# GpSimd takes two products of VectorE in a hybrid decoder layer: the delta rule's gate and the rotation's sin

## The chip, the cores and the metric

One core of one Trainium2 chip runs the whole program. The metric is the device time of one execution in microseconds. Single numbers below come from one profiled execution, whose own time stands beside its span.

## The reference, cut to what matters

Two decoder layers run over 576 token columns: 512 of a prompt and 64 of eight sampled sequences. Each layer projects the normed input and feeds three token mixers: a gated linear recurrence (RG-LRU), sparse attention (NSA) and a gated delta rule. The change touches the output of the delta rule and the rotation of q and k of the attention.

```python
q = rope(rmsnorm(nsa_q...), pos) * HD ** -0.5        # 8 heads of 64
k = rope(rmsnorm(kv[:, :, 0::2], k_norm), pos)       # 3 branches, 2 heads of 64
# rope on the first 16 of each head's 64:
concat([x1 * c - x2 * s, x2 * c + x1 * s, rest])
...
o_dn = rmsnorm(o_dn, dn_o_norm)
out_dn = (o_dn * silu(dn_z)) @ w_dn_out
```

## The kernel before, in words

Columns of features lie on the 128 partitions and the 576 tokens along the free dimension, all in float32. Five engines run their own instruction lists and meet through semaphores.

TensorE carries one long list of dense units (`UNITS`, 288 token columns of one product each). Their order is fixed, and `fill(n, end)` strews n matmuls of it between the small matmuls of the mixers; each unit writes one of two PSUM banks in turn, so a unit can start only when the one two before it has been evicted. Weights are multiplied in a seven-product scheme (`PRODUCTS = "1627543"`): VectorE forms sums of weight quarters in SBUF (`weight_sums`, three instructions, after product 5; `weight_sum`, one instruction, after product 6), and both inputs of these lie in SBUF. VectorE evicts most units in `take_to(end)`, which handles all units up to `end`; `take_before(name, count)` evicts up to what TensorE had been given when it reached that step. Both are in order: what stands behind an instruction on VectorE waits for it.

Between the delta rule and attention each layer goes through this stretch:

- `times_roots` (L1984) multiplies the norms in, out of PSUM, for o (the delta rule's output, `dc[:, 0:4]`), then k (`qk7[:, 4:7]`), then q (`qk7[:, 0:4]`), each in two halves of 288 tokens. `bm_ok` counts them: 6 when o is done, 8 when k is, 10 when q is. TensorE's broadcasts for the next norm wait for them.
- GpSimd (L829 to L834) waits for `bm_ok` 8 and 10 and issues four DMAs each, which write the rows of k and q with the two rotation halves swapped into `rs7`. They count `nk_sw` and `nq_sw`.
- VectorE, after `bm_ok` 10, multiplies `zs[:, 8:12]` (the SiLU gate) with `dc[:, 0:4]`, 2304 elements per partition (`dn_ok`). Then for k (1728 elements) and q (2304): the swapped rows times sin, the rows times cos, and their sum (`qk_ok` 1 and 2), with evictions in between.
- TensorE waits for `bm_ok` 10, then for 16 matmuls of dense work later for `qk_ok` 1, and transposes k and v in five tiles with dense work in between (L864). ScalarE copies them out of PSUM to `ktok` (L1714), from where GpSimd writes them to DRAM (L840 to L848).
- SyncE loads the cached keys of the first samples after `dn_ok` and `qk_ok` 2 (L659).

The helpers that most instructions go through have lines of their own in the trace: `mul` is L1799, `add` L1802, `sub` L1805, matmuls of the dense list L935, transposes L864, norm broadcasts L981. `arena`, `zs`, `ring`, `ws`, `sg` and `con` are in SBUF, `PS` is PSUM; `dc`, `qk7`, `rs7` and the tables of sin and cos are parts of `arena`.

Of the kernel before, what the change touches and what calls it, by code (L numbers as in the profile page):

```python
# [16 lines left out]
ALU = mybir.AluOpType  # L17
# [278 lines left out]
NORMS = {"dn": (0, 4), "dn_k": (1, 4), "o": (2, 4), "k": (3, 3), "q": (4, 4)}  # L296


def chained(eng, done):
# [12 lines left out]
CON_IN = 16 * 3  # L312
# [7 lines left out]
qb_ok ck_in wk_in cv_in s_pl s_pe s_kt s_ke s_t s_ed s_ea s_sg s_sc s_pv s_cm s_ce  # L320
s_cn s_im s_wc s_m s_mw s_wm s_sm s_p s_pw s_tr s_tb s_ta s_mix s_or s_ot s_z dh_t
conv_ok silu_ok dc_ok sp_abs sp_exp gb_ok bm_ok s0_in p_z p_y p_g p_e p_x p_s p_d p_k p_b i_w
# [5 lines left out]
    par_in=192, lrow_in=48, par_t=1, ssq_ok=1, x_ps=1, rt_ok=5, rr_ok=5, xn_ok=5, x_t=9, sq_ok=19, ms_ok=5, rstd_ok=5,  # L328
    h_ok=9, lam_ok=1, lh_t=1, u_ok=4, lgp=8, lg=8, at_ok=1, lt_ok=1, lq_ok=1, lru_ok=1, lc_ok=1, lc_in=1, lo_t=2,
    lo_ok=3, gt_t=1, gt_ok=2, gs_ok=2, bc_ok=10, nk_sw=64, nq_sw=64, qk_ok=2, kt_t=5, kt_e=5, vc_mm=1, c_ok=1, c_s=4,  # L330
    c_m=4, c_e=4, c_t=4, c_c=4, c_pv=4, c_n=4, a_s=64, a_m=64, a_p=64, a_r=32, a_n=64, a_t=40, a_ca=20, a_cd=20,
    a_v=40, z_o=4, qb_ok=3, ck_in=1024, wk_in=128, cv_in=1152, s_pl=4, s_pe=4, s_kt=4, s_ke=4, s_t=24, s_ed=12,
    s_ea=12, s_sg=4, s_sc=4, s_pv=4, s_cm=4, s_ce=4, s_cn=4, s_im=4, s_wc=4, s_m=4, s_mw=4, s_wm=4, s_sm=4, s_p=4,
    s_pw=4, s_tr=8, s_tb=4, s_ta=4, s_mix=4, s_or=4, s_ot=4, s_z=8, dh_t=1, conv_ok=12, silu_ok=6, dc_ok=1, sp_abs=2,
    sp_exp=3, gb_ok=1, bm_ok=10, s0_in=128, p_z=5, p_y=5, p_g=20, p_e=5, p_x=5, p_s=5, p_d=5, p_k=15, p_b=5, i_w=31,
# [5 lines left out]
def hybrid_trunk(nc, dram, out):  # L341

    ctx = ExitStack()
    with ctx:
# [5 lines left out]
        zs = sb("zs", [P, 12, T])  # L350
# [152 lines left out]
        def rep(ap, n):  # L503

            return ap.unsqueeze(1).to_broadcast([ap.shape[0], n, ap.shape[1]])
# [258 lines left out]
        def _(pool):  # L764
            pool.memset(wab, 0.0).then_inc(s["zero"], 1)
            pool.memset(gtok[:], 0.0).then_inc(s["zero"], 1)
            for l in range(DEPTH):
# [55 lines left out]
                for h in range(DN_H):  # L823
# [4 lines left out]
                               S0.rearrange("p b h e -> p (b h) e")).then_inc(s["b_out"], 16)  # L828

                for norm, landed_rows, n, m in (("k", "nk_sw", 4, 7), ("q", "nq_sw", 0, 4)):  # L830
                    pool.wait_ge(s["bm_ok"], past["bm_ok"] + 2 * NORMS[norm][0] + 2)
                    for at in (0, HD):
                        for to, of in ((at, at + ROT // 2), (at + ROT // 2, at)):
                            pool.dma_start(rs7[to:to + ROT // 2, n:m], qk7[of:of + ROT // 2, n:m]).then_inc(s[landed_rows], 16)  # L834
                pool.wait_ge(s["b_out"], l * 32 + 32)
                for k, (t, n) in enumerate(TILES):
# [23 lines left out]
        def _(pe):  # L860
# [145 lines left out]
            for l in range(DEPTH):  # L1006
# [15 lines left out]
                for c in range(12):  # L1022
                    ins = turn(PS[:, 3, c * 24:(c + 1) * 24], drow[:, c * P:(c + 1) * P])
                ins.then_inc(s["dh_t"], 1)
                dense_to(u0 + SM_END + 2)
# [468 lines left out]
        def _(act):  # L1494
# [32 lines left out]
            for l in range(DEPTH):  # L1527
# [39 lines left out]
                def take_before(name, count):  # L1567

                    take_to(began[(name, past[name] + count)])
# [140 lines left out]
                for k, (t, n) in enumerate(TILES):  # L1710
                    take_before("kt_t", k + 1)
                    act.wait_ge(s["kt_t"], past["kt_t"] + k + 1)
                    b = 4 + 2 * (k % 2)
                    A(ktok[0:n, k, :], PS[0:n, b:b + 2, :].rearrange("p b n -> p (b n)")[:, 0:6 * P], ACT.Copy)\  # L1714
                        .then_inc(s["kt_e"], 1)
# [78 lines left out]
        def _(dve):  # L1794
# [3 lines left out]
            def mul(dst, a, b):  # L1798
                return V.tensor_tensor(dst, a, b, ALU.mult)  # L1799
# [47 lines left out]
            for l in range(DEPTH):  # L1847
# [121 lines left out]
                def take_before(name, count):  # L1969

                    take_to(began[(name, past[name] + count)])
# [20 lines left out]
                V.tensor_copy(h0[:], rows[:, :, 24:32])  # L1992
                dve.wait_ge(s["dh_t"], past["dh_t"] + 1)
                link(V.tensor_copy(dhist, PS[:, 3, 0:12 * 24]))
# [211 lines left out]
                dve.wait_ge(s["bm_ok"], past["bm_ok"] + 10)  # L2206
                dve.wait_ge(s["silu_ok"], past["silu_ok"] + 5)
                mul(zs[:, 8:12], zs[:, 8:12], dc[:, 0:4]).then_inc(s["dn_ok"], 1)
                normed = began[("bc_ok", past["bc_ok"] + 10)]
                take_to(normed + 1)  # L2210
                dve.wait_ge(s["con_in"], CON_IN * (l + 1))
                for landed_rows, n, m in (("nk_sw", 4, 7), ("nq_sw", 0, 4)):
                    dve.wait_ge(s[landed_rows], past[landed_rows] + 64)
                    x, y = qk7[:, n:m], rs7[:, n:m]
                    link(mul(y, y, rep(C("sin"), m - n)))
                    if n == 0:
                        take_before("kt_t", 2)
                    else:
                        take_to(normed + 2)
                    link(mul(x, x, rep(C("cos"), m - n)))  # L2220
                    if n == 0:
                        take_before("kt_t", 3)
                    else:
                        take_to(normed + 3)
                    add(x, x, y).then_inc(s["qk_ok"], 1)
                    take_before("kt_t", 1 if n else 4)
# [203 lines left out]
```

## Time and profile before

| | |
|---|---|
| median of 3 runs | 1876.11 us (1875.68 to 1879.31) |
| profiled execution | 1875.9 us, of which the span is 1874.1 us |
| TensorE busy | 1815.8 us, 97% |
| VectorE busy | 963.7 us, 51% |
| ScalarE busy | 517.1 us, 28% |
| GpSimd busy | 90.6 us, 5% |
| mean granted TensorE clock | 0.993 of full |

Busy shares are means over the whole span. TensorE's hardly drops below nine tenths in any slice of the page, so what another engine costs must be read from the places where TensorE waits for it. An execution has each stretch twice, once per layer, some 929 us apart.

### The profile page before, as it was taken

Reading aid. Unit: us, or ns where it says so; the run is one execution under the profiler, and the core shown is the slowest. Engines: PE = TensorE matmul, PEld = TensorE weight load, DVE = VectorE, ACT = ScalarE, POOL = GpSimd, SP = SyncE. Lnnn points to the kernel's source line nnn. Section 1 sums busy time; section 2 is a strip of 40 time slices with the busy share of each in tenths; the row PEclk is TensorE's granted clock in tenths of the full one; section 3 lists DMA queues with packets and bytes.
Section 4 is the critical chain, followed back from the end, with each engine's and each line's share of the span. In section 5 each row is a group of like instructions: output and inputs, shape, how many; then the busy total and the mean of one; then the engine's idle time right before and its main releaser. Section 6 shows DMA issues by size and latency. Waiting matters only on the chain.

```text
span 1874.1 us, 29566 instructions
## 1 busy us (share of the span) xinstructions
PE 1815.8 (97%) x11454; PEld 1300.3 (69%) x11454; DVE 963.7 (51%) x2246; ACT 517.1 (28%) x1161; POOL 90.6 (5%) x133
## 2 busy tenths in 40 slices
PE   7999999999899999999999999999998999999999
PEld 5777788886665577676467777888866555777763
DVE  2749554534765555533137595555347565555321
ACT  3142412013256612200112424020142565221100
POOL 0000201001200000000000002010012000000000
PEclk9999999998999999999999999999999999999999
DMA  6312402023341035645042232021144311464411
GB/s 212 99 45 68 118 25 46 24 63 111 107 133 35 26 115 157 186 126 172 0 162 68 67 85 79 24 46 54 32 133 122 97 34 35 131 194 127 157 73 40
DMA packets 196529, 170.08 MB, mean 91 GB/s; under 512 B 49248, under 2 KB 186898, under 8 KB 195942
## 3 DMA queue, kind: packets, MB, share of 16 engines
q1 hardware_dynamic: 192164, 150.11, 27.2%
q0 software_dynamic: 4064, 18.03, 3.0%
q8 instruction: 91, 1.49, 0.3%
q14 instruction: 48, 0.39, 0.1%
q10 hardware_dynamic: 162, 0.05, 0.0%
HBM read 153.67 MB, written 21.71 MB: 94 GB/s over the span
## 4 chain that ended last, share of the span: by engine, by line
PE 81%; DVE 11%; issue 3%; SPq 2%; ACT 2%; DMA 1%; ACTq 0%; DVEq 0%
PE PS L935 53%; PE PS L864 6%; DVE arena L1874 3%; PE PS L1308 2%; PE PS L1321 2%; PE PS L1156 2%; PE PS L1138 1%; PE PS L1158 1%; DVE arena L1799 1%; PE PS L1377 1%; SPq L652 1%; PE PS L1227 1%; PE PS L1041 1%; PE PS L1249 1%; PE PS L1170 1%
## 5 line engine op out<-in xcount | busy, mean ns | idle before, releaser
L935 PE MATMUL PS<-hT,ring 128*128 128x288 f32 x2384 | 631.9, 410 | 3.8 <-DVE arena L1915 2.3
L935 PEld LDWEIGHTS PS<-hT,ring 128*128 128x128 f32 x2384 | 441.0, 190 | 132.2 <-issue 12.0
L935 PE MATMUL PS<-tt,ws 128*128 128x288 f32 x736 | 207.3, 414 | 10.6 <-DVE sg L1932 4.3
L935 PE MATMUL PS<-zs,owr 128*128 128x288 f32 x768 | 208.0, 413 | 6.4 <-DVE sg L1805 4.2
L935 PEld LDWEIGHTS PS<-zs,owr 128*128 128x128 f32 x768 | 139.4, 191 | 49.8 <-issue 12.4
L935 PEld LDWEIGHTS PS<-tt,ws 128*128 128x128 f32 x736 | 132.4, 190 | 55.0 <-issue 9.2
L864 PE MATMUL PS<-con,arena 128*128 128x128 f32 (+5 forms) x934 | 145.3, 282 | 13.7 <-DMA arena<-in_nsa_k_norm 10.1
L864 PEld LDWEIGHTS PS<-con,arena 128*128 128x128 f32 (+5 forms) x934 | 108.4, 141 | 72.4 <-issue 42.2
L1802 DVE TENSOR_TENSOR sg<-PS,sg 128x288 f32<-128x288 f32 x140 | 63.9, 457 | 139.9 <-PE PS L935 138.6
L935 PE MATMUL PS<-arena 128*128 128x512 f32 (+1 forms) x320 | 124.8, 593 | 2.1 <-DVE sg L1932 2.1
L935 PE MATMUL PS<-tt,ring 128*128 128x288 f32 x368 | 107.1, 424 | 0.0
L1874 DVE SCALAR_TENSOR_TENSOR arena<-arena,par 128x512 f32<-128x512 f32 x192 | 99.4, 518 | 6.3
L935 PEld LDWEIGHTS PS<-arena 128*128 128x128 f32 (+1 forms) x320 | 52.8, 179 | 71.0 <-issue 68.1
L1558 ACT ACTIVATE sg<-PS 128x288 f32<-128x288 f32 x46 | 18.6, 404 | 260.2 <-PE PS L935 260.0
L1732 ACT ACTIVATE arena<-PS,sm 128x128 f32<-128x128 f32 (+3 forms) x128 | 66.9, 524 | 69.1 <-DVE sm L2283 63.2
L935 PEld LDWEIGHTS PS<-tt,ring 128*128 128x128 f32 x368 | 68.8, 196 | 20.6 <-issue 2.6
L2283 DVE CUSTOM_DVE_ANT_0 PS<-PS,con 128x128 f32<-128x128 f32 (+3 forms) x128 | 61.8, 505 | 40.2 <-PE PS L1308 40.2
L1805 DVE TENSOR_TENSOR arena<-arena,PS 128x512 f32<-128x512 f32 (+3 forms) x70 | 43.3, 621 | 56.8 <-PE PS L1158 36.7
L1723 ACT ACTIVATE arena<-arena,sm 128x128 f32<-128x128 f32 (+3 forms) x128 | 64.7, 553 | 23.2 <-DVE sm L1799 23.2
L1799 DVE TENSOR_TENSOR arena<-arena 128x2304 f32<-128x2304 f32 (+3 forms) x24 | 39.7, 1654 | 58.1 <-ACT arena L1613 22.2
L1965 DVE SCALAR_TENSOR_TENSOR arena<-PS,arena 128x512 f32<-128x512 f32 x18 | 12.4, 691 | 103.9 <-PE PS L935 97.2
L1805 DVE TENSOR_TENSOR ws<-ring 128x512 f32<-128x512 f32 x92 | 63.3, 688 | 3.1 <-DMA ring<-in_w_in 1.5
(306 smaller groups left out, 2159.6 us busy)
## 6 DMA issues: line engine op xcount, KB each, us to landing
ring<-in_w_in SPq DMA_DIRECT2D x54, 1024.0 KB, 5.3
arena<-in_cache_nsa_kv SPq DMA_DIRECT2D x128, 192.0 KB, 2.6
ring<-in_w_in SPq DMA_DIRECT2D x32, 256.0 KB, 4.3
arena<-in_state_nsa_win SPq DMA_DIRECT2D x32, 256.0 KB, 3.3
arena<-in_cache_nsa_kv SPq DMA_DIRECT2D x128, 64.0 KB, 1.8
arena<-in_w_out SPq DMA_DIRECT2D x4, 2048.0 KB, 8.2
out_win_sample<-in_state_nsa_win POOLq DMA_DIRECT2D x2, 4032.0 KB, 23.0
arena<-in_x_prompt SPq DMA_DIRECT2D x8, 512.0 KB, 5.6
```

The lines of the kernel that those rows point to most:

```text
L864: return nc.tensor.transpose(dst, src, ident[0:src.shape[0], 0:src.shape[0]])
L935: ins = mm(to, w, x, start=start, stop=stop, skip_group_check=True)
L1156: mm(new[0][m], Y[m, h, m], blocks(w[m], sz, 0), start=True, stop=True)
L1308: mm(PS[:, 4 + g, 0:q0 + P], qk7[m, r, q0:q0 + P], qk7[m, 5 + br, 0:q0 + P], start=True, stop=True).then_inc(s["a_s"], 1)
L1321: ins = mm(PS[g * HD:(g + 1) * HD, 7, rp * 2 * P:(rp + 1) * 2 * P], ktok[:, kb, col:col + HD], pTring[j % 2][:, g * 2 * P:(g + 1) * 2 * P] ...
L1723: A(p, p, ACT.Copy, scale=sm8[:, 7, u % 8:u % 8 + 1]).then_inc(s["a_n"], 1)
L1732: A(pring[slot % PRING][:, 0:width], PS[:, 4 + slot % 2, 0:width], ACT.Exp, scale=-1.0, bias=sm8[:, 0, k:k + 1], accum_out=sm8[:, 1, k:k + ...
L1799: return V.tensor_tensor(dst, a, b, ALU.mult)
L1802: return V.tensor_tensor(dst, a, b, ALU.add)
L1805: return V.tensor_tensor(dst, a, b, ALU.subtract)
L1874: ins = stt(out=d, in0=e, scalar=w(j), in1=d, op0=ALU.mult, op1=ALU.add)
L2283: V.tensor_tensor_reduce(out=raw, in0=raw, in1=C("causal")[:, 3 * P - q0:4 * P], scale=-1.0, scalar=-NEG, op0=ALU.add, op1=ALU.min, accum_ ...
```

## The change

GpSimd makes the product of `zs[:, 8:12]` and `dc[:, 0:4]` as soon as the o norm is done, ahead of its row-swapping DMAs, and after these DMAs it multiplies the swapped rows of k and then of q by sin. VectorE keeps the products with cos and the sums, and waits for `sn_ok` before a sum. One eviction step (`take_to(normed + 3)` for k, `take_before("kt_t", 3)` for q) that stood between cos and the sum is gone. ScalarE waits for `dn_ok` before its first copy to `ktok`, which shares its memory with `dc`. The semaphore `dh_t` is folded into `lh_t`, which frees one for `sn_ok`.

```diff
@@ gpsimd @@
+                pool.wait_ge(s["bm_ok"], past["bm_ok"] + 2 * NORMS["o"][0] + 2)
+                pool.wait_ge(s["silu_ok"], past["silu_ok"] + 5)
+                nc.gpsimd.tensor_tensor(zs[:, 8:12], zs[:, 8:12], dc[:, 0:4], ALU.mult).then_inc(s["dn_ok"], 1)
                 for norm, landed_rows, n, m in (("k", "nk_sw", 4, 7), ("q", "nq_sw", 0, 4)):
                     pool.wait_ge(s["bm_ok"], past["bm_ok"] + 2 * NORMS[norm][0] + 2)
                     for at in (0, HD):
                         for to, of in ((at, at + ROT // 2), (at + ROT // 2, at)):
                             pool.dma_start(rs7[to:to + ROT // 2, n:m], qk7[of:of + ROT // 2, n:m]).then_inc(s[landed_rows], 16)
+                pool.wait_ge(s["con_in"], CON_IN * (l + 1))
+                for landed_rows, n, m in (("nk_sw", 4, 7), ("nq_sw", 0, 4)):
+                    pool.wait_ge(s[landed_rows], past[landed_rows] + 64)
+                    nc.gpsimd.tensor_tensor(rs7[:, n:m], rs7[:, n:m], rep(C("sin"), m - n), ALU.mult).then_inc(s["sn_ok"], 1)
@@ tensor @@
-                ins.then_inc(s["dh_t"], 1)
+                ins.then_inc(s["lh_t"], 1)
@@ scalar @@
                     take_before("kt_t", k + 1)
+                    if k == 0:
+                        act.wait_ge(s["dn_ok"], past["dn_ok"] + 1)
                     act.wait_ge(s["kt_t"], past["kt_t"] + k + 1)
@@ vector @@
-                dve.wait_ge(s["dh_t"], past["dh_t"] + 1)
+                dve.wait_ge(s["lh_t"], past["lh_t"] + 2)
...
                 dve.wait_ge(s["bm_ok"], past["bm_ok"] + 10)
-                dve.wait_ge(s["silu_ok"], past["silu_ok"] + 5)
-                mul(zs[:, 8:12], zs[:, 8:12], dc[:, 0:4]).then_inc(s["dn_ok"], 1)
                 normed = began[("bc_ok", past["bc_ok"] + 10)]
                 take_to(normed + 1)
                 dve.wait_ge(s["con_in"], CON_IN * (l + 1))
                 for landed_rows, n, m in (("nk_sw", 4, 7), ("nq_sw", 0, 4)):
                     dve.wait_ge(s[landed_rows], past[landed_rows] + 64)
                     x, y = qk7[:, n:m], rs7[:, n:m]
-                    link(mul(y, y, rep(C("sin"), m - n)))
+                    link(mul(x, x, rep(C("cos"), m - n)))
                     if n == 0:
                         take_before("kt_t", 2)
                     else:
                         take_to(normed + 2)
-                    link(mul(x, x, rep(C("cos"), m - n)))
-                    if n == 0:
-                        take_before("kt_t", 3)
-                    else:
-                        take_to(normed + 3)
+                    dve.wait_ge(s["sn_ok"], past["sn_ok"] + (1 if n else 2))
                     add(x, x, y).then_inc(s["qk_ok"], 1)
                     take_before("kt_t", 1 if n else 4)
```

## Rows read from the trace of the kernel before

**Rows 1.** The page: the chain that ended last, shares of the span by engine.
```profile
PE 81%; DVE 11%; issue 3%; SPq 2%; ACT 2%; DMA 1%; ACTq 0%; DVEq 0%
```

**Rows 2.** Chain of waits, 470 to 525 us: start, us, what.
```profile
486.22 1.42 DVE arena L1984
...
496.79 0.46 DVE sg L1805
```

**Rows 3.** Timeline of VectorE, layer 0: start, us, engine, line, operation, [idle before <- releaser].
```profile
476.53 1.41 DVE L1984 SCALAR_TENSOR_TENSOR arena<-arena,par,PS 128x1152 f32<-128x1152 f32 x1
...
480.91 0.68 DVE L1805 TENSOR_TENSOR ring<-ring,ws 128x512 f32<-128x512 f32 x1
...
486.22 1.41 DVE L1984 SCALAR_TENSOR_TENSOR arena<-arena,par,PS 128x1152 f32<-128x1152 f32 x1 [0.97 <-PE PS L981]
...
487.67 2.56 DVE L1799 TENSOR_TENSOR zs<-zs,arena 128x2304 f32<-128x2304 f32 x1
...
490.51 1.95 DVE L1799 TENSOR_TENSOR arena<-arena 128x1728 f32<-128x1728 f32 x1
...
492.87 0.68 DVE L1805 TENSOR_TENSOR ws<-ring 128x512 f32<-128x512 f32 x1
...
505.30 2.55 DVE L1802 TENSOR_TENSOR arena<-arena 128x2304 f32<-128x2304 f32 x1
```

**Rows 4.** Timeline of TensorE, layer 0.
```profile
493.01 2.21 PE L935 MATMUL PS<-hT,ring 128*128 128x288 f32 x8
...
497.30 2.29 PE L935 MATMUL PS<-zs,owr 128*128 128x288 f32 x4 [2.08 <-DVE sg L1805]
...
500.66 2.12 PE L935 MATMUL PS<-zs,owr 128*128 128x288 f32 x8
```

**Rows 5.** Timeline of TensorE, layer 1.
```profile
1416.33 1.24 PE L935 MATMUL PS<-tt,ws 128*128 128x288 f32 x4 [1.52 <-DVE arena L1984]
...
1425.93 1.24 PE L935 MATMUL PS<-zs,owr 128*128 128x288 f32 x4 [2.08 <-DVE sg L1805]
...
1428.51 2.11 PE L935 MATMUL PS<-zs,owr 128*128 128x288 f32 x8
```

**Rows 6.** Source lines L824, L805, L834 on GpSimd: ns min/median/max, landings in us.
```profile
L824 POOL TENSOR_TENSOR arena<-arena x8: 1900/1902/1906, 430.3 to 1364.7; 128x1024 f32<-128x1024 f32 x8
...
L805 POOL COPY arena<-con x10: 604/1037/1042, 217.2 to 1322.1; 128x1024 f32<-128x1024 f32 x8, 64x512 f32<-64x512 f32 x2
...
DMA to landing us min/median/max: 2.0/2.4/4.5
```

**Rows 7.** Timeline, GpSimd and VectorE where they overlap or not.
```profile
200.53 0.74 DVE L1805 TENSOR_TENSOR ws<-ring 128x512 f32<-128x512 f32 x1
...
203.46 0.60 POOL L799 TENSOR_SCALAR arena<-con,gtok 128x128 f32<-128x128 f32 x1
...
223.39 1.26 POOL L799 TENSOR_SCALAR arena<-con,gtok 128x128 f32<-128x128 f32 x1 [4.20 <-PE PS L1105]
...
223.58 0.68 DVE L1799 TENSOR_TENSOR arena<-arena 128x512 f32<-128x512 f32 x1
...
434.17 0.46 DVE L1805 TENSOR_TENSOR zs<-sg,PS 128x288 f32<-128x288 f32 x1 [3.61 <-PE PS L935]
```

**Rows 8.** Timeline of GpSimd: the swapped rows' DMAs, layer 0.
```profile
483.16 2.04 POOL L834 DMA_DIRECT2D arena<-arena  x4 [25.16 <-DVE arena L1984]
...
487.93 1.98 POOL L834 DMA_DIRECT2D arena<-arena  x4 [2.73 <-DVE arena L1984]
```

**Rows 9.** Windows of 5 us: length, busy us by engine, PEclk, DMA share, GB/s.
```profile
425.00:430.00 5.00, 5.00 (x28) 5.00 (x28) 0.00 (x0) 0.00 (x0) 0.00 (x0) 0.56 0.00 0
...
430.00:435.00 5.00, 5.00 (x14) 3.59 (x14) 0.88 (x2) 0.00 (x0) 4.74 (x3) 0.50 0.00 0
...
495.00:500.00 5.00, 2.92 (x8) 1.98 (x8) 4.96 (x5) 0.00 (x0) 0.00 (x0) 0.73 0.68 210
...
500.00:505.00 5.00, 5.00 (x27) 4.17 (x26) 4.93 (x4) 2.29 (x4) 1.56 (x3) 0.93 0.23 82
```

More of the change, by code:

```diff
@@ L320 @@
 qb_ok ck_in wk_in cv_in s_pl s_pe s_kt s_ke s_t s_ed s_ea s_sg s_sc s_pv s_cm s_ce
-s_cn s_im s_wc s_m s_mw s_wm s_sm s_p s_pw s_tr s_tb s_ta s_mix s_or s_ot s_z dh_t
+s_cn s_im s_wc s_m s_mw s_wm s_sm s_p s_pw s_tr s_tb s_ta s_mix s_or s_ot s_z sn_ok
 conv_ok silu_ok dc_ok sp_abs sp_exp gb_ok bm_ok s0_in p_z p_y p_g p_e p_x p_s p_d p_k p_b i_w
@@ L328 @@
     par_in=192, lrow_in=48, par_t=1, ssq_ok=1, x_ps=1, rt_ok=5, rr_ok=5, xn_ok=5, x_t=9, sq_ok=19, ms_ok=5, rstd_ok=5,
-    h_ok=9, lam_ok=1, lh_t=1, u_ok=4, lgp=8, lg=8, at_ok=1, lt_ok=1, lq_ok=1, lru_ok=1, lc_ok=1, lc_in=1, lo_t=2,
-    lo_ok=3, gt_t=1, gt_ok=2, gs_ok=2, bc_ok=10, nk_sw=64, nq_sw=64, qk_ok=2, kt_t=5, kt_e=5, vc_mm=1, c_ok=1, c_s=4,
+    h_ok=9, lam_ok=1, lh_t=2, u_ok=4, lgp=8, lg=8, at_ok=1, lt_ok=1, lq_ok=1, lru_ok=1, lc_ok=1, lc_in=1, lo_t=2,
+    lo_ok=3, gt_t=1, gt_ok=2, gs_ok=2, bc_ok=10, nk_sw=64, nq_sw=64, sn_ok=2, qk_ok=2, kt_t=5, kt_e=5, vc_mm=1, c_ok=1, c_s=4,
     c_m=4, c_e=4, c_t=4, c_c=4, c_pv=4, c_n=4, a_s=64, a_m=64, a_p=64, a_r=32, a_n=64, a_t=40, a_ca=20, a_cd=20,
@@ L333 @@
     s_ea=12, s_sg=4, s_sc=4, s_pv=4, s_cm=4, s_ce=4, s_cn=4, s_im=4, s_wc=4, s_m=4, s_mw=4, s_wm=4, s_sm=4, s_p=4,
-    s_pw=4, s_tr=8, s_tb=4, s_ta=4, s_mix=4, s_or=4, s_ot=4, s_z=8, dh_t=1, conv_ok=12, silu_ok=6, dc_ok=1, sp_abs=2,
+    s_pw=4, s_tr=8, s_tb=4, s_ta=4, s_mix=4, s_or=4, s_ot=4, s_z=8, conv_ok=12, silu_ok=6, dc_ok=1, sp_abs=2,
     sp_exp=3, gb_ok=1, bm_ok=10, s0_in=128, p_z=5, p_y=5, p_g=20, p_e=5, p_x=5, p_s=5, p_d=5, p_k=15, p_b=5, i_w=31,
```

## The prediction

> **What bounds the kernel now.** I read the page first. TensorE is busy for 97% of the span and the chain that ended last is 81% TensorE and 11% VectorE [rows 1]. An edit on VectorE and GpSimd therefore counts only where TensorE waits for them, and there it counts at full length. The next view is the chain of waits in the stretch that the change touches, once per layer: it is on VectorE at 486.22 us, when the last half of the q norm is multiplied in (L1984), and still there at 496.79 us, the eviction that lets TensorE go on at 497.30 [rows 2, 4]. The timeline of VectorE shows what it does there in order: the product of the delta rule's output with its gate (2.56 us), an eviction, sin on k (1.95), an eviction with three sums of weights (0.69 each, the first at 492.87), cos on k, an eviction, the sum for k [rows 3]. TensorE's timeline shows what is late: it ends a unit at 495.22, sits 2.08 us for VectorE's L1805, starts the next at 497.30, and after the first transposes of k goes on densely from 500.66 [rows 4]. Layer 1 is the same picture: 1416.33, 1425.93, 1428.51 [rows 5]. From there on the q half of the rotation lies beside dense TensorE work. So a layer can win at most the idle time of this stretch, some 3 us.
>
> **The price of the moved products.** GpSimd's only two-input product in the trace takes 1.90 us for 1024 elements [rows 6], 1.86 ns each, against 2.56 us for 2304, 1.11 ns each, on VectorE [rows 3]. By the row: 2304 x 1.86 = 4.28 us for the gate product and for sin on q, 1728 x 1.86 = 3.21 us for sin on k. That row's second operand repeats one number over 128 elements, so it may flatter. From above I bound the price by two one-input passes (a copy of 1024 is 1.04 us [rows 6]): 4.7 and 3.5 us. From below by one pass: 2.3 and 1.8. I take the row, as the nearest.
> The Trainium skill (GPSIMD Engine Reference, section 3.1) measured 4497 ns for such an addition of 2048 elements. An estimate by that page is 5.06 and 3.79 us, and would put some 2.3 us per layer on the sum below. No run here shows it.
>
> **Can both engines work at once?** This decides. I looked at every GpSimd instruction that overlaps VectorE. The 128x128 tensor_scalar takes 0.60 us alone (203.46), but 1.26 us at 223.39, where VectorE runs a 0.68 us instruction with both inputs in SBUF (arena<-arena, 223.58): it is longer by that instruction [rows 7]. Of the 40 instructions of L799, eight (four per layer) overlap a VectorE instruction with two SBUF inputs, and these eight alone are stretched. Beside instructions whose one input is in PSUM nothing is stretched: the four products from 430.26 keep their 1.90 us with 434.17 beside them [rows 6, 7]. The other direction shows once per layer: the weight sum at 200.53, whose start met a waiting GpSimd instruction, took 0.74 us instead of 0.68 or 0.69 [rows 3, 7], about the short read of 128 elements. So each waits for the other, and I take it that a long GpSimd product holds VectorE as long as it reads.
> The Trainium skill says just this (SBUF — State Buffer, section Who interferes with whom): a VectorE instruction with two SBUF inputs and a GpSimd instruction that reads SBUF exclude each other for a whole instruction, whoever comes first. The trace agrees for GpSimd, +0.66 us, and shows the other direction only at +0.05 us.
>
> **Step 1, the gate product.** It needs the o norm (476.53 + 1.41 = 477.94) and comes first in GpSimd's queue. GpSimd wakes 0.29 us after such a product (486.22 + 1.41 = 487.63, its DMAs at 487.93) [rows 3, 8]: 478.23 to 482.5. VectorE has a weight sum (ring<-ring,ws, 0.68 us, both inputs in SBUF) at 480.91 [rows 3]. It is held to 482.5 and hands over at about 483.1 instead of 481.6. Behind it in the queue stands the k norm, for which TensorE and GpSimd's k DMAs wait. Cost: +1.5 us. With a GpSimd that lets VectorE pass it is 0. Once the q norm is done (D), TensorE is free in both kernels; D moves from 487.63 to 489.13.
>
> **Step 2, the k half, counted from D.** VectorE no longer has the 2.56 us product: it evicts TensorE's first unit (done at 1.3) to 1.8 and makes cos on k to 3.7. GpSimd issues the q DMAs from 0.3 to 2.3 [rows 8], starts sin on k at 2.3, is held to 3.7, and needs 3.0 us more: 6.7. The k rows have landed by then (issued before D, 2.4 us to landing [rows 6]). VectorE evicts to 4.15; its three weight sums read SBUF twice, and the first is held to 6.7. The first two run back to back, to 8.0. The third waits for the second by semaphore, and there GpSimd, now with sin on q in hand, gets in, as it did between the sums at 200.53. Its 4.0 us of reading hold the third sum to 12.0. Then: third sum 12.7, sum for k 14.6, the eviction that was ahead of it and now comes behind it 15.05, and TensorE starts the next unit at 15.1. Before, that was 497.30 - 487.63 = 9.67: +5.4 us.
>
> **Step 3, given back behind it.** The k sum is then long done, so unit and transposes run in 1.7 us at full clock, where it was 3.36 us in layer 0 (500.66 - 497.30, at the lower clock, below) and 2.58 in layer 1 [rows 4, 5]. That gives back 1.6 and 0.9.
>
> **Step 4, the clock.** TensorE idled about 2.1 us before 497.30 and the granted clock was 0.73 and 0.93 of full in the two slices from 495 to 505, that is 3.4 us at 1.2 GHz instead of 2.4. From 425 to 435 us, under sparse small matmuls, the clock stood at 0.56 and 0.50 [rows 9]. The new idle time is about 7.5 us, so I count 3.4 us at the lower level per layer once it resumes: +1.7 us each, between 0 and 5 (all of such a stretch of ten).
>
> **Costs of nothing.** The q half ends at about D + 21.1 = 510.2 (evictions to 15.5, cos q 18.1, eviction 18.5, sum 21.1), 2.4 us later than before (505.30 + 2.55 = 507.85) [rows 3]. The cached-key loads on SP that wait for it move by less than TensorE does; if they were needed at once they would cost those 2.4 us. ScalarE's new wait for the gate product (done at 482.5) stands before work of 500 us. GpSimd's output DMAs queue behind its sin on q (501.1), and their first was issued when the first transposed rows were out, which moves later. The merged semaphore changes no instruction. Each hidden by TensorE's own work.
>
> **Sum.** Layer 0: 1.5 + 5.4 - 1.6 + 1.7 = 7.0. Layer 1: 1.5 + 5.4 - 0.9 + 1.7 = 7.7. Together +14.7 us. The profiled execution took 1875.9 us (span 1874.1 and 1.8 around it), 0.2 below the median of 1876.11. The sum gives 1890.6 by the one, 1890.8 by the other: 1891. Own range: 1884 (no clock loss, -3.4; sin on q gets the port only behind the k sum and holds cos on q instead, which costs TensorE about 1.5 us less per layer, -3) to 1902 (prices from above, +1.1 per layer; the low clock at its 5 us, +3.3 per layer; the cached keys needed at once, +2.4).
>
> **Rivals.**
> *VectorE is never held, GpSimd alone yields.* For: the long delays in the trace are all GpSimd's. Against: 0.74 us. Step 1 costs 0. Sin on k starts at D + 2.3, yields to cos (3.7) and to the sums (2.0 us of them) and ends at about 8.8; the k sum ends at 10.8, the next unit starts at 11.3 instead of 9.67, and 1.7 us later the transposes are done: 13.0 against 13.03 in layer 0 and 12.2 in layer 1. About +1 us in all: 1877, no change. Chance 0.13.
> *The other side: the products are hidden.* Both engines run freely. Sin on k is done at D + 5.5, the weight sums at 6.3, the k sum at 8.2, eviction 8.7, transposes done 10.4: -2.6 us in layer 0, -1.8 in layer 1, 1871.7 us, faster by 0.24%. It decides as long as sin on k ends before the weight sums do, at D + 6.3. For it: VectorE's own work shrinks by 2 x 7 us. Against: the stretched rows. Chance 0.09.
> *As forecast, VectorE held by GpSimd:* 0.78.
>
> **The numbers.** A measurement here tells a change from none at about 0.2%, 3.75 us. Slower 0.78, same 0.13, faster 0.09. The range leaves out the hidden case (0.09) below and reaches from the no-change case, less the scatter of a run, to the upper end of the forecast's own range: 1875 to 1902.
>
> **What would show it.** In the trace after: the gate product on GpSimd at about 4.3 us and, beside it, the weight sum of 480.91 stretched to about 2.2 us; the first weight sum behind cos on k stretched to about 3 us and the third to about 4; the next unit at D + 15; TensorE idle for 7 us in one piece and a clock slice at 0.5 behind it. If the weight sums keep 0.69 us, step 1 and 2 are wrong and the time stays at or below 1877. If GpSimd takes 5 us per product, the time lies near 1896. If sin on q gets in elsewhere, step 2 changes by up to 4 us.

## The result, and the profile after

The changed kernel takes 1898.42 us (median of 4 runs, 1896.48 to 1902.69) against 1876.54 for the kernel before: ratio 1.0118, 95% interval 1.0106 to 1.0131. It is 22 us slower; 1891 was forecast, with a range of 1875 to 1902. The profiled execution took 1896.48 us, its span is 1894.6 us, 20.5 more than before, and the mean granted clock went from 0.993 to 0.987 of full.

GpSimd's timeline after, layer 0 (start, us, engine, line, operation):
```profile
477.84 5.06 POOL L832 TENSOR_TENSOR zs<-zs,arena 128x2304 f32<-128x2304 f32 x1 [20.03 <-DVE arena L1993]
...
491.78 3.85 POOL L841 TENSOR_TENSOR arena<-arena 128x1728 f32<-128x1728 f32 x1
495.81 6.54 POOL L841 TENSOR_TENSOR arena<-arena 128x2304 f32<-128x2304 f32 x1 [0.19 <-DMA arena<-arena]
```
VectorE's, with `mul` now at L1808, `add` L1811, `sub` L1814, `times_roots` L1993:
```profile
480.72 2.73 DVE L1814 TENSOR_TENSOR ring<-ring,ws 128x512 f32<-128x512 f32 x1
...
488.08 1.41 DVE L1993 SCALAR_TENSOR_TENSOR arena<-arena,par,PS 128x1152 f32<-128x1152 f32 x1 [0.97 <-PE PS L988]
...
491.26 6.19 DVE L1808 TENSOR_TENSOR arena<-arena 128x1728 f32<-128x1728 f32 x1
497.49 0.46 DVE L1811 TENSOR_TENSOR sg<-PS,sg 128x288 f32<-128x288 f32 x1
497.86 5.04 DVE L1814 TENSOR_TENSOR ws<-ring 128x512 f32<-128x512 f32 x1
...
511.79 2.55 DVE L1811 TENSOR_TENSOR arena<-arena 128x2304 f32<-128x2304 f32 x1
```
Three VectorE instructions carry the whole change: the weight sum of 480.72 (0.68 us in [rows 3]), cos on k (1.95 there) and the first of the three weight sums (0.68 there). Each meets one of GpSimd's three products and ends only behind it: at 483.45 behind 482.90, at 497.45 behind 495.63, at 502.90 behind 502.35. GpSimd is held once too: sin on q begins 1.6 us before the end of cos on k and takes 6.54 us instead of the 5.06 of the gate product, which has as many elements. All other VectorE instructions of the stretch keep their lengths.

TensorE's timeline, layer 0: first the line of the kernel before for its first unit behind the q norm, which [rows 4] leave out,
```profile
487.69 1.24 PE L935 MATMUL PS<-tt,ws 128*128 128x288 f32 x4 [1.52 <-DVE arena L1984]
```
then the changed kernel, which answers to [rows 4]:
```profile
489.55 1.24 PE L942 MATMUL PS<-tt,ws 128*128 128x288 f32 x4 [1.52 <-DVE arena L1993]
...
498.00 4.21 PE L942 MATMUL PS<-hT,ring 128*128 128x288 f32 x8 [3.33 <-DVE sg L1811]
506.52 2.29 PE L942 MATMUL PS<-zs,owr 128*128 128x288 f32 x4 [4.31 <-DVE sg L1814]
...
509.88 2.41 PE L942 MATMUL PS<-zs,owr 128*128 128x288 f32 x8
```
and layer 1, to [rows 5]:
```profile
1427.70 1.24 PE L942 MATMUL PS<-tt,ws 128*128 128x288 f32 x4 [1.54 <-DVE arena L1993]
...
1444.69 2.29 PE L942 MATMUL PS<-zs,owr 128*128 128x288 f32 x4 [4.31 <-DVE sg L1814]
...
1448.05 2.65 PE L942 MATMUL PS<-zs,owr 128*128 128x288 f32 x8
```
The unit is the first on `zs,owr`, at 497.30 in [rows 4] and at 506.52 here. Where one wait of 2.08 us stood ahead of it there are two, 3.33 us for the eviction behind cos and 4.31 us for the one behind the k sum. Windows of 5 us (length, busy us by engine, granted clock, DMA share, GB/s), to [rows 9]:
```profile
495.00:500.00 5.00, 2.00 (x4) 1.51 (x5) 4.97 (x3) 0.44 (x1) 4.81 (x2) 0.68 0.00 0
500.00:505.00 5.00, 2.20 (x5) 1.01 (x3) 4.97 (x4) 0.00 (x0) 2.36 (x1) 0.50 0.32 77
505.00:510.00 5.00, 3.48 (x11) 2.81 (x12) 4.38 (x4) 0.00 (x0) 0.00 (x0) 0.50 0.40 136
510.00:515.00 5.00, 5.00 (x26) 3.97 (x26) 3.29 (x3) 2.29 (x4) 2.11 (x4) 0.95 0.23 80
...
1420.00:1425.00 5.00, 3.60 (x14) 2.19 (x14) 2.67 (x4) 0.41 (x1) 2.10 (x4) 0.68 0.25 46
```
**Accounting, layer 0.** D, the end of the q norm, is 488.08 + 1.41 = 489.49 instead of 487.63, +1.9, and so is the start of TensorE's first unit behind it (489.55 - 487.69). TensorE came into the stretch 0.19 us early in this execution, so the stretch itself added 2.05. From D to the unit at 506.52: 17.03 us instead of 9.67, +7.4. From there to the next dense unit 509.88 - 506.52 = 3.36, as before, and +0.3 in that unit (2.41 against 2.12). Together +9.7. **Layer 1:** D comes later by 3.7 relative to the matmuls ahead of it, then +7.4, then 3.36 against 2.58 (+0.8), then 2.65 against 2.11 (+0.5): +12.4. The sum is 22.1. TensorE gains 1.6 us elsewhere in this execution, most of it near 1365 us, where a stretch at the lower clock falls otherwise than before; 20.5 is left, the difference of the spans.

### The profile page after: what moved, and what is told of

Its sections match the earlier page's. It is cut to its first block, busy times and chain, and to the rows that moved or that the text cites. A ratio compares the mean times of both kernels' runs of the same rounds, so it can differ in the third digit from the quotient of the medians.

```text
span 1894.6 us, 29570 instructions
## 1 busy us (share of the span) xinstructions
PE 1821.5 (96%) x11454; PEld 1304.1 (69%) x11454; DVE 971.8 (51%) x2240; ACT 517.1 (27%) x1161; POOL 121.7 (6%) x139
## 4 chain that ended last, share of the span: by engine, by line
PE 82%; DVE 11%; issue 3%; ACT 2%; SPq 2%; DMA 0%; ACTq 0%; DVEq 0%
PE PS L942 53%; PE PS L871 6%; DVE arena L1883 3%; PE PS L1315 2%; PE PS L1328 2%; DVE arena L1808 2%; PE PS L1163 1%; PE PS L1145 1%; PE PS L1165 1%; PE PS L1384 1%; DVE ws L1814 1%; PE PS L1234 1%; PE PS L1048 1%; PE PS L1256 1%; SPq L652 1%
## 5 line engine op out<-in xcount | busy, mean ns | idle before, releaser
L942 PE MATMUL PS<-hT,ring 128*128 128x288 f32 x2384 | 635.7, 412 | 10.1 <-DVE sg L1811 6.7
L942 PEld LDWEIGHTS PS<-hT,ring 128*128 128x128 f32 x2384 | 443.0, 191 | 139.4 <-issue 11.9
L942 PE MATMUL PS<-zs,owr 128*128 128x288 f32 x768 | 209.9, 415 | 10.1 <-DVE sg L1814 8.6
L942 PE MATMUL PS<-tt,ws 128*128 128x288 f32 x736 | 208.2, 415 | 10.8 <-DVE sg L1941 4.4
L942 PEld LDWEIGHTS PS<-zs,owr 128*128 128x128 f32 x768 | 140.5, 193 | 54.7 <-issue 11.6
L942 PEld LDWEIGHTS PS<-tt,ws 128*128 128x128 f32 x736 | 133.0, 191 | 55.5 <-issue 9.4
L1811 DVE TENSOR_TENSOR sg<-PS,sg 128x288 f32<-128x288 f32 x140 | 64.0, 457 | 142.7 <-PE PS L942 141.0
L942 PE MATMUL PS<-arena 128*128 128x512 f32 (+1 forms) x320 | 124.8, 593 | 2.1 <-DVE sg L1941 2.1
L942 PE MATMUL PS<-tt,ring 128*128 128x288 f32 x368 | 106.4, 422 | 0.0
L942 PEld LDWEIGHTS PS<-arena 128*128 128x128 f32 (+1 forms) x320 | 52.7, 179 | 71.1 <-issue 68.1
L942 PEld LDWEIGHTS PS<-tt,ring 128*128 128x128 f32 x368 | 68.8, 196 | 20.3 <-issue 2.6
L1814 DVE TENSOR_TENSOR ws<-ring 128x512 f32<-128x512 f32 x92 | 72.0, 783 | 3.4 <-DMA ring<-in_w_in 1.7
L1814 DVE TENSOR_TENSOR arena<-arena,PS 128x512 f32<-128x512 f32 (+3 forms) x70 | 43.3, 621 | 56.6 <-PE PS L1165 36.7
L1808 DVE TENSOR_TENSOR arena<-arena 128x2304 f32<-128x2304 f32 (+3 forms) x20 | 39.2, 1960 | 58.1 <-ACT arena L1620 22.2
L1545 ACT ACTIVATE sg<-sg 128x288 f32<-128x288 f32 x72 | 31.2, 436 | 127.3 <-DVE sg L1811 112.2
```

The lines of the kernel that those rows point to most:

```text
L942: ins = mm(to, w, x, start=start, stop=stop, skip_group_check=True)
L1545: A(sg[:, place], sg[:, place], ACT.Tanh, scale=0.5).then_inc(s["th_ok"], 1)
L1811: return V.tensor_tensor(dst, a, b, ALU.add)
L1814: return V.tensor_tensor(dst, a, b, ALU.subtract)
```

## The experiments

Ratios are to the kernel before, timed beside it on the same chip: 1877.7 to 1878.2 us. A layer's D is the end of its q norm, as above.

### One half of the change at a time

`e1_gate_only` keeps GpSimd's gate product and gives sin back to VectorE in the old order:
```diff
-                    nc.gpsimd.tensor_tensor(rs7[:, n:m], rs7[:, n:m], rep(C("sin"), m - n), ALU.mult).then_inc(s["sn_ok"], 1)
...
+                    link(mul(y, y, rep(C("sin"), m - n)))
```


> GpSimd makes the gate product only; sin stays on VectorE in the order of before. Theory P (GpSimd's reads of SBUF and VectorE instructions with two SBUF inputs shut each other out): the weight sum beside the gate product is stretched to about 2.7 us, the end of the q norm comes 2.05 us later, and VectorE wins about 1.2 us per layer behind it because the 2.56 us product is gone: +0.9 us per layer, 1878 us, up to 1882 with a low-clock stretch. Theory S (the loss is waiting for GpSimd's slow results): nothing waits for the gate product, so only the gain shows: 1874 us.

`e2_sin_only` does the reverse, with the gate product on VectorE again, behind the q norm:
```diff
-                nc.gpsimd.tensor_tensor(zs[:, 8:12], zs[:, 8:12], dc[:, 0:4], ALU.mult).then_inc(s["dn_ok"], 1)
...
+                mul(zs[:, 8:12], zs[:, 8:12], dc[:, 0:4]).then_inc(s["dn_ok"], 1)
```


> GpSimd makes the two sin products only; the gate product is VectorE's. Theory P: cos on k is stretched beside sin on k, the first weight sum behind it beside sin on q (to about 5 us), the next unit starts some 17.4 us behind the end of the q norm instead of 9.7: +8 us per layer, 1892 us. Theory S: the k sum waits for sin on k, which is done about 6.1 us behind the end of the q norm, before VectorE comes to the sum: no loss, 1876 us or less.

Measured: 1879.83 us, ratio 1.0020 (1.0007 to 1.0032), and 1894.72 us, ratio 1.0091 (1.0070 to 1.0112). Both lie near what theory P gave (1878 and 1892) and far from theory S (1874 and 1876). The sin products make nearly eight tenths of the loss, +17.0 of +21.9 us; the gate product makes +2.1, and 2.7 us are in neither. TensorE's timeline of `e1_gate_only`:
```profile
486.63 2.12 PE L938 MATMUL PS<-tt,ws 128*128 128x288 f32 x4
...
491.55 1.24 PE L938 MATMUL PS<-tt,ws 128*128 128x288 f32 x4 [1.55 <-DVE arena L1989]
...
500.04 1.24 PE L938 MATMUL PS<-zs,owr 128*128 128x288 f32 x4 [1.43 <-DVE sg L1810]
```
From TensorE's start behind D to the unit is 8.5 us (500.04 - 491.55), 1.1 less than before (497.30 - 487.69), since VectorE is rid of the product. But D is late by more than the held weight sum: the clock granted from 485 to 490 is 0.66, and the four matmuls of 486.63 take 2.12 us instead of 1.13. TensorE had idled 2.22 us just ahead of that, for VectorE.

VectorE's timeline of `e2_sin_only`, cos on k and the first weight sum:
```profile
490.96 5.22 DVE L1805 TENSOR_TENSOR arena<-arena 128x1728 f32<-128x1728 f32 x1
...
496.59 5.05 DVE L1811 TENSOR_TENSOR ws<-ring 128x512 f32<-128x512 f32 x1
```
The same two are held. Here GpSimd's sin on k was first (490.36, 4.01 us), so cos waited for it from its own start. TensorE's timeline of the same run:
```profile
488.13 1.24 PE L939 MATMUL PS<-tt,ws 128*128 128x288 f32 x4 [1.53 <-DVE arena L1990]
...
505.25 2.29 PE L939 MATMUL PS<-zs,owr 128*128 128x288 f32 x4 [4.94 <-DVE sg L1811]
```
From its start behind D to the unit are 17.1 us with the gate product on VectorE, and 17.0 in the changed kernel without it (506.52 - 489.55). So what VectorE wins by giving the product away, 1.1 us in `e1_gate_only`, is all but gone once sin is on GpSimd. That is some 2 of the 2.7 us.

### Is it what GpSimd reads, or that it is late?

`e3_writes_only` replaces each product by a chain of memsets of about its length. They write the same tiles and read nothing; the gate product and the sin products are left out of the computation. Of each chain the diff shows that for sin.
```diff
-                nc.gpsimd.tensor_tensor(rs7[:, n:m], rs7[:, n:m], rep(C("sin"), m - n), ALU.mult).then_inc(s["sn_ok"], 1)
+                    for i, w in enumerate((T, T, 200)):
+                        pool.memset(rs7[:, n:m, 0:w], 0.0).then_inc(s["sn_ok"], 1)
```


> GpSimd's three products are replaced by chains of memsets over the same tiles that last about as long, so the gate product and sin are left out, but every semaphore comes at about the same time. Theory P: writes alone shut nothing out, no VectorE instruction is stretched, the next unit starts about 8.6 us behind the end of the q norm: 1873 us. Theory S: the results come as late as in the changed kernel, so the time stays near 1898 us. A variant of P in which GpSimd's writes count as well: VectorE stretched, near 1890 us.

`e4_four_columns` leaves GpSimd 4 of the 576 columns of each product; the rest is left out.


> GpSimd's products cover 4 of 576 token columns (the rest of gate product and sin is left out); all waits and the order of all queues stay as in the changed kernel. Theory P and S alike: 1871.7 us, the case of the hidden products. Theory Q (the new order of evictions and waits itself costs time): above 1876 us.

Measured: 1872.37 us, ratio 0.9976 (0.9966 to 0.9985), and 1872.75 us, ratio 0.9977 (0.9967 to 0.9988). GpSimd's, then VectorE's timeline of `e3_writes_only`:
```profile
490.28 3.81 POOL L844 MEMSET arena<- 128x1728 f32 x3
494.38 4.92 POOL L844 MEMSET arena<- 128x2304 f32 x3 [0.29 <-DMA arena<-arena]
```
```profile
489.79 1.95 DVE L1812 TENSOR_TENSOR arena<-arena 128x1728 f32<-128x1728 f32 x1
491.77 0.46 DVE L1815 TENSOR_TENSOR sg<-PS,sg 128x288 f32<-128x288 f32 x1
492.14 0.68 DVE L1818 TENSOR_TENSOR ws<-ring 128x512 f32<-128x512 f32 x1
```
GpSimd is occupied for as long as with the products, VectorE waits for it at the same semaphores, and nothing is stretched. Without GpSimd's reads the change would win 5 us; with them it loses 22. `e4_four_columns` says the same of the new order of evictions and waits: by itself it costs nothing. The Trainium skill (SBUF — State Buffer, section Who interferes with whom) says that a VectorE instruction with two SBUF inputs contends with GpSimd's reads and not with its writes: the trace agrees, at 3.81 us of writes beside 1.95 and 0.68.

`e3_writes_only` also gives the prediction's second step without contention: from D (488.03) to the unit (496.50) is 8.47 us. Add what the two held instructions lost, 6.19 - 1.95 = 4.24 and 5.04 - 0.68 = 4.36, and the 17.03 of the changed kernel is there: 17.07.

### Less to read

`e8_half_columns` makes GpSimd's products over 288 of 576 columns, the other half left out.


> The changed kernel, with GpSimd's three products made over the first 288 of 576 columns alone; the other half of each product is left out. GpSimd should take 2.53 us for the gate product and 1.93 and 2.5 us for the sin products. P (what GpSimd reads is what VectorE waits for, in proportion): the weight sum beside the gate product keeps 0.68 us, the cos product of the keys is stretched from 1.95 to about 4.2 us (6.19 with the whole product), the first weight sum behind it to about 2.6 us (5.04 with the whole); the unit begins some 4.5 us earlier than in the changed kernel, and the weight sum gives 2 us: 6.5 less in each layer, 1885 us, ratio 1.004, between 1.001 and 1.007. F (the one that began first keeps the path, and a short GpSimd product only waits, as with 4 columns): no VectorE product is stretched by over 0.3 us, 1873 us, ratio 0.998.

Measured: 1884.95 us, ratio 1.0039 (1.0023 to 1.0054). VectorE's timeline:
```profile
489.18 4.36 DVE L1808 TENSOR_TENSOR arena<-arena 128x1728 f32<-128x1728 f32 x1
...
493.94 2.77 DVE L1814 TENSOR_TENSOR ws<-ring 128x512 f32<-128x512 f32 x1
```
As theory P had it: the delay goes with what GpSimd reads (4.36 expected as 4.2, 2.77 as 2.6). The weight sum beside the gate product kept 0.68 us, also as expected: GpSimd's half product (477.80, 2.62 us) ended just before it began (480.68).

### Who is held

In the changed kernel cos on k began first (491.26), GpSimd's sin on k 0.52 us later, and yet VectorE was held: 3.85 us for GpSimd, then the rest of cos. In `e4_four_columns` VectorE was first by the same 0.52 us, and GpSimd's read of 12 elements took 1.51 us, to the end of cos; 16 elements, met by nothing, took 0.21. Four kernels went after that. The first shifts GpSimd's read by five small memsets ahead of it, the last by two:
```diff
                 pool.wait_ge(s["con_in"], CON_IN * (l + 1))
+                for i in range(5):
+                    pool.memset(kcp[:], 0.0).then_inc(s["sn_ok"], 1)
+                    pool.wait_ge(s["sn_ok"], past["sn_ok"] + i + 1)
```


> The changed kernel, with five small memsets of a spare tile on GpSimd, each waiting for the one before, between its row DMAs and its sin product of the keys: GpSimd's first read of the rotation begins some 1 us later, when VectorE has been in its cos product of the keys for 1 us or more (0.5 us in the changed kernel). Two accounts of who is held. H (the engine that began first keeps its data path for the whole of its instruction): the cos product takes its own 1.95 us, GpSimd's sin product of the keys takes 3.85 plus what is left of the cos product (4.5 to 5), and the first weight sum (0.68 alone) is held behind it to 3 us or more. I (GpSimd's read gets in during VectorE's instruction): the cos product is stretched again, to 5.5 to 6.5 us, and the sin product of the keys takes 3.85. Either way GpSimd reads as much as in the changed kernel and 1 us later: 1896 to 1902 us, ratio to the kernel before 1.010 to 1.014.

> The changed kernel with two of the small memsets instead of five ahead of GpSimd's sin product of the keys, whole products: its read begins about 0.9 us into the cos product of the keys (0.52 with none: VectorE held from there; 1.46 with five: GpSimd held 0.4 us, until the cos product had ended). R (an engine gets in wherever the other is, unless it is all but done): cos product 5.5 to 6.3 us, sin product 3.8 to 3.9. L (only early in the other's instruction): cos product 1.95 us, sin product of the keys about 4.8. Time 1897 to 1902 us.

The other two make the products over 24 and over 96 columns, the rest left out.

> The changed kernel with GpSimd's three products over the first 24 of 576 columns alone, the rest of them left out. Its sin product of the keys has 72 elements a partition, about 0.35 us by itself, and begins 0.5 us into VectorE's cos product of the keys. With 12 elements it was held until that product's end; with 864 and 1728 it got in and VectorE was held. Z (short reads are held, the bound lies above 72 elements): cos product 1.95 us, GpSimd's product about 1.5 us. Y (the bound lies below): cos product about 2.4 us or more, GpSimd's product 0.35 to 0.5. Time about 1873 us in either.

> The same with 96 of 576 columns: 288 elements a partition, about 0.8 us by itself. Z (288 elements are held as 12 were): cos product 1.95 us, GpSimd's product 2.1 to 2.3 us. Y (they get in as 864 did): cos product about 2.8 to 3 us, GpSimd's 0.8 to 0.9. Time 1873 to 1877 us.

Measured: `e6_later_reads` 1900.61 us, ratio 1.0126 (1.0111 to 1.0141); the others, run once each, `e12_reads_later_by_half` 1900.70, `e10_24_columns` 1873.75 and `e11_96_columns` 1876.89 us. VectorE's timeline of `e6_later_reads`, cos on k and the first two weight sums:
```profile
492.77 1.95 DVE L1811 TENSOR_TENSOR arena<-arena 128x1728 f32<-128x1728 f32 x1
...
495.13 3.84 DVE L1817 TENSOR_TENSOR ws<-ring 128x512 f32<-128x512 f32 x1
498.90 5.52 DVE L1814 TENSOR_TENSOR ring<-ring 128x512 f32<-128x512 f32 x1
```
and GpSimd's, which began 1.46 us into cos:
```profile
494.23 4.20 POOL L844 TENSOR_TENSOR arena<-arena 128x1728 f32<-128x1728 f32 x1
```
GpSimd's in `e12_reads_later_by_half`, 0.90 us into a cos of 1.95:
```profile
494.53 4.75 POOL L844 TENSOR_TENSOR arena<-arena 128x1728 f32<-128x1728 f32 x1
```
Now cos is whole and GpSimd is held, by 0.4 and 0.9 us. The cost moves to the two weight sums behind cos, which take 3.84 and 5.52 us in `e6_later_reads` instead of 0.68: 8.0 us held, against 8.6 in the changed kernel. In `e11_96_columns` (VectorE, then GpSimd, 0.53 us apart) GpSimd gets in again, against theory Z:
```profile
490.53 3.15 DVE L1808 TENSOR_TENSOR arena<-arena 128x1728 f32<-128x1728 f32 x1
```
```profile
491.06 0.81 POOL L841 TENSOR_TENSOR arena<-arena 128x288 f32<-128x288 f32 x1
```
In `e10_24_columns` its 72 elements, 0.52 us into cos, cost VectorE 0.14 us and took 1.76 us themselves, to just behind the end of cos. In layer 1 of that kernel its second product began 0.11 us into VectorE's k sum and was held for all of it:
```profile
1420.07 2.09 POOL L841 TENSOR_TENSOR arena<-arena 128x96 f32<-128x96 f32 x1 [2.25 <-DMA arena<-arena]
```
Whenever GpSimd got in, VectorE was longer by GpSimd's time and 0.39 us: 6.19 - 1.95 - 3.85, 4.36 - 1.95 - 2.02, 3.15 - 1.95 - 0.81. What sets these cases apart from the others is not which engine began first, nor simply by how much. At 0.11, 0.23, 0.29, 0.90 and 1.46 us into VectorE's instruction GpSimd was held; at 0.51 to 0.54 it got in, but for reads of 72 elements or fewer. It may be what GpSimd came from: wherever it got in it came straight from issuing the row DMAs, and in the five others from a memset or from idling on a semaphore. That is not enough either: in `e2_sin_only` it came from the same DMAs, 2.24 us into VectorE's gate product of 2.56 us (0.3 us before its end), and was held by some 0.15 us. None of this was tried by itself, and it stays open. The Trainium skill's section named above calls the shared port pair an exclusive lock, says that issue order decides who blocks and, of another mode of VectorE's, that whoever issues first gets the pair for the whole instruction. The five meetings in which GpSimd was held agree; cos on k of the changed kernel, of `e8_half_columns` and of `e11_96_columns` does not.

### The place of the work, with nothing on GpSimd

If 22 us hang on the engine and `e3_writes_only` won 5 without VectorE's products, how much is to be had by order alone? `e5_gate_late` is the kernel before with the gate product behind the k sum:
```diff
-                dve.wait_ge(s["silu_ok"], past["silu_ok"] + 5)
-                mul(zs[:, 8:12], zs[:, 8:12], dc[:, 0:4]).then_inc(s["dn_ok"], 1)
...
                     add(x, x, y).then_inc(s["qk_ok"], 1)
+                    if n:
+                        take_before("kt_t", 1)
+                        dve.wait_ge(s["silu_ok"], past["silu_ok"] + 5)
+                        mul(zs[:, 8:12], zs[:, 8:12], dc[:, 0:4]).then_inc(s["dn_ok"], 1)
+                        take_before("kt_t", 2)
```
and ScalarE's first copy to `ktok` waits for `dn_ok`, as in the changed kernel.


> All work stays on VectorE, as in the kernel before; only its place changes: the gate product of the delta rule (2.57 us on VectorE) is made after the sum of the rotated keys instead of ahead of the last normalisation's output unit, and ScalarE's first copy of key tokens, which reads it, waits for it. P (the place of the gate product is worth something, the engine is not): in layer 0 the product lay between the end of the q norm (D) and the next output unit of TensorE, which before began at D + 9.67 us; without its 2.57 us there, with the wait for the row DMAs (issued about 1 us before) taking up part of it, the unit begins at about D + 8.5, 1.2 us earlier in each layer: 1877.7 less 2.4 = 1875.3, ratio 0.9987, held between 0.9975 and 1.0. No VectorE instruction between 470 and 520 us is longer than in the kernel before. S (VectorE's load there does not bound the unit, the row DMAs do): the sin product of the keys begins no earlier than before, ratio 1.000 +- 0.0005.

`e7_gate_and_sums_late` also puts the three weight sums behind that product.


> As the run with the late gate product, and the three weight sums that VectorE makes between the rotation's products (0.68 us each) also wait until behind the gate product. Nothing is on GpSimd. P: the two sin and cos products of the keys, their sum and the key transposes come without anything between them; the next output unit begins at about D + 7.4 instead of D + 9.7, and the first transposes of rotated keys at about D + 8.5 instead of D + 11.6; 3.1 us earlier in each of two layers: 1877.7 less 6.2 = 1871.5, ratio 0.9967, between 0.994 and 0.999. S (the deferred sums are needed by TensorE's dense units sooner than that): TensorE waits for a weight sum in the dense units behind, and the gain is cut to that of the late gate product alone, ratio 0.998 to 1.000.

`e9_evictions_between` is that one with two eviction steps moved up, between sin and cos of q and between cos and the sum:
```diff
-                        take_before("kt_t", 3)
+                        take_before("kt_t", 4)
...
-                        take_before("kt_t", 4)
+                        take_before("kt_t", 5)
```


> As the run with the late gate product and weight sums, and VectorE takes the evictions of the dense units ahead of the fourth and fifth key transposes between and behind the two products of the queries, instead of behind both. P (in that run TensorE waited 1.40 us in layer 0 for the eviction that stood behind 5.14 us of two query products, and that cost the rest of its gain): that wait is gone, 1.4 us in each of two layers, 1874.0 less 2.8 = 1871.2, ratio to the kernel before 0.9965, between 0.995 and 0.998. S (the wait is made good by the next stage anyway): ratio 0.998 to 0.999, as without the edit.

Measured: 1874.34 us, ratio 0.9986 (0.9977 to 0.9995); 1873.95 us, 0.9982 (0.9973 to 0.9991); 1875.83 us, 0.9990 (0.9981 to 0.9999). The first is as expected, the second won 3.7 us of 6.2, and the third, which should have won the rest, won none of it. TensorE's timeline of `e7_gate_and_sums_late`:
```profile
486.39 1.24 PE L935 MATMUL PS<-tt,ws 128*128 128x288 f32 x4 [1.53 <-DVE arena L1989]
...
493.29 1.13 PE L935 MATMUL PS<-zs,owr 128*128 128x288 f32 x4
494.82 0.88 PE L864 MATMUL PS<-con,arena 128*128 128x128 f32 x6 [0.40 <-DVE arena L1804]
...
505.86 1.24 PE L935 MATMUL PS<-hT,ring 128*128 128x288 f32 x4 [1.40 <-DVE arena L1932]
...
531.72 1.21 PE L935 MATMUL PS<-zs,owr 128*128 128x288 f32 x4 [1.06 <-DMA owr<-in_w_lru_out]
```
From TensorE's start behind D (486.39 here, 487.69 before) the unit comes after 6.9 us instead of 9.6, and the transposes after 8.4 instead of 11.7: 2.7 and 3.3 us are won, a little more than expected. (That TensorE stands 4.0 us earlier at the unit than in [rows 4] is in part that it came to D 1.3 us earlier in this execution.) The 1.40 us at 505.86 are the wait that `e9_evictions_between` removes, and it is gone there. But in layer 0 TensorE then meets a load of output weights that it did not wait for before. In `e9_evictions_between` it waits 2.80 us for it:
```profile
488.30 1.24 PE L935 MATMUL PS<-tt,ws 128*128 128x288 f32 x4 [1.53 <-DVE arena L1989]
...
533.48 1.21 PE L935 MATMUL PS<-zs,owr 128*128 128x288 f32 x4 [2.80 <-DMA owr<-in_w_lru_out]
```
SyncE's timeline of that kernel shows why, 16 loads of cached keys ahead of it in the queue:
```profile
512.12 16.83 SPq L659 DMA_DIRECT2D arena<-in_cache_nsa_kv  x16
...
529.47 1.05 SPq L635 DMA_DIRECT2D owr<-in_w_lru_out  x2
```
and of the kernel before:
```profile
509.61 17.50 SPq L659 DMA_DIRECT2D arena<-in_cache_nsa_kv  x16
...
528.06 1.05 SPq L635 DMA_DIRECT2D owr<-in_w_lru_out  x2
```
The cached keys wait for the q sum. Counted from TensorE's start behind D (487.69, 486.39, 488.30) it ended after 20.2 us before, 21.9 in `e7_gate_and_sums_late` and 22.2 in `e9_evictions_between`: what is moved behind the k half is ahead of the q half, and delays the weights by way of SyncE's queue. Counted in the same way, the unit that needs them began after 46.1, 45.3 and 45.2 us: of the 3.3 us that layer 0 had won at the transposes, 0.7 and 0.9 are left.

Another part of the loss is the clock. Windows of 5 us show it, first two of `e7_gate_and_sums_late`, then two of `e9_evictions_between`:
```profile
1450.00:1455.00 5.00, 3.11 (x14) 1.64 (x13) 3.40 (x18) 2.73 (x11) 0.00 (x0) 0.86 0.61 183
1455.00:1460.00 5.00, 5.00 (x24) 3.41 (x24) 2.31 (x9) 2.27 (x8) 0.00 (x0) 0.80 0.67 194
```
```profile
535.00:540.00 5.00, 5.00 (x20) 2.59 (x18) 2.00 (x11) 2.07 (x8) 0.00 (x0) 0.70 0.66 203
...
1455.00:1460.00 5.00, 5.00 (x24) 2.90 (x21) 1.91 (x11) 2.45 (x11) 0.00 (x0) 0.66 0.72 202
```
The kernel before has a granted clock of 1.00 in all of these. Behind the wait of 2.80 us, with the clock at 0.70, `e9_evictions_between` loses 1.6 us more. In layer 1 neither version waits for the weights, and each loses 1.4 us in the stretch shown; the idle time of 1.9 us just ahead of it, for ScalarE, is in the kernel before too, where the clock stayed up. These are single executions, and how often the clock falls there was not counted.

## Why the prediction was right, and where its sum fell short

**The side and the mechanism were right.** GpSimd's reads hold VectorE's instructions with two SBUF inputs, and TensorE waits for them at full length: shown by `e3_writes_only` and `e8_half_columns`. VectorE never held (1877) and both running freely (1871.7) are out. What the second rival priced, the change without contention, came out at -5.3 us where it had -4.4.

**The price of the products was mis-sized.** By the row of 1024 elements they were to take 4.28 and 3.21 us; they took 5.06 and 3.85. Sin on q took 6.54 us with what it was held. The row did flatter, by a fifth, and the bound from two one-input passes (4.7 and 3.5) did not hold either. The estimate by the Trainium skill (GPSIMD Engine Reference, section 3.1), 5.06 and 3.79, was met, and the prediction said that GpSimd at 5 us per product would put the time near 1896. (It put 2.3 us per layer on that; by its own terms, two products of 0.78 us more and one of 0.58, it is 2.1.)

**The reading of the stretched rows** left out one thing. GpSimd's instruction at 223.39, read as held by the one of 223.58 alone, had begun 0.42 us into a weight sum ahead of that (222.97, 0.69 us). It already stood waiting, and VectorE's next instruction still went before it.

**Step 1** expected the weight sum held to about 2.2 us and D +1.5. It took 2.73 us and D came +2.05 in layer 0. In layer 1 it was +3.7: TensorE idled 2.22 us for it, and the granted clock was 0.68 from 1420 to 1425. The four matmuls of L942 there took 2.04 us instead of 1.13. The clock had been counted behind the k half alone; a short idle time ahead of D costs as much.

**Step 2** expected +5.4 and got +7.4 in both layers, by another path. It had GpSimd yield to cos on k and then hold the first and the third weight sum. In fact cos itself was interrupted, the first weight sum met sin on q, and the third kept 0.69 us. Two instructions were held in either version, so the wrong path cost little: for 2.55 + 4.0 us in the prediction, for 4.24 + 4.36 in the trace. Of these 2.05 us more the longer products are 1.4, and handing over the port in the middle of cos is 0.39. TensorE's idle time came in two pieces, 3.33 and 4.31 us, and not in one of 7.

**Steps 3 and 4** expected -1.6 (-0.9 in layer 1) given back at full clock and +1.7 for 3.4 us at the lower level. In layer 0 the clock stood at 1.2 GHz for some 13.7 us (0.68, 0.50, 0.50, 0.95 in the four windows), four times as long. Most of that lay under TensorE's waits: the unit of 498.00 took 4.21 instead of 2.10 us and still ended before VectorE was ready. What showed is that nothing was given back: 3.36 us as before, and +0.3 behind it, against +0.1 for the two steps together. In layer 1 it was +1.3 against +0.8.

**Sum:** 7.0 and 7.7 expected, 9.7 and 12.4 measured, 1.6 given back elsewhere. **Costs of nothing** held in the changed kernel, where TensorE is later than all it might have waited for. The q sum ended at 514.34, 6.5 us later than before and not 2.4, but TensorE was 9.5 us late. The cost of nothing does not hold once TensorE is early: the q sum sets the weight load that cut the gain of layer 0 in `e7_gate_and_sums_late` and `e9_evictions_between`.

## What to carry to other kernels

Before giving GpSimd an elementwise product of two SBUF tiles, list the VectorE instructions with both inputs in SBUF that will run beside it: in this case each that met one lost up to the whole of GpSimd's time, which is twice what VectorE would have needed for the product, and where GpSimd was held the loss only went to VectorE's next such instruction. What GpSimd only wrote cost nothing here. The gain that the edit aimed at was a matter of place: the same work on VectorE, put where TensorE doesn't wait for it, won 0.10 to 0.18%. More was lost again to the next queue behind it (here SyncE's, by the q sum) and to the clock.

## What was not expected of the hardware

- GpSimd got in 0.5 us after VectorE had begun, and stopped a 1.95 us instruction in the middle for 0.81, 2.02 or 3.85 us, with 0.39 us on top each time. At 0.9 and 1.46 us in, coming from a memset, it was held.
- A GpSimd read of 12 elements beside VectorE was held for its neighbour's whole rest: 1.51 us, where 16 elements alone took 0.21.
- The same idle time of 2.22 us ahead of a norm's broadcast was followed by a granted clock of 0.66 in `e1_gate_only` (485 to 490 us) and 0.68 in layer 1 of the changed kernel (1420 to 1425), but left it at 1.00 in layer 0 of the changed kernel (485 to 490). What TensorE did just before was the same list of matmuls; what decides is open.
